# Joining the quarters of a Strassen-like MLP in PSUM, rectifying and squaring them on ScalarE, and spreading the modulation chunks anew

## What is computed

```python
def squared_relu_mlp(h, w_in, w_out):
    return jnp.square(jax.nn.relu(h @ w_in)) @ w_out
...
for i in range(DEPTH):
    ml = jnp.split((c_act @ w_mod[i] + b_mod[i])[:, None, :], 6, axis=-1)
    mc = jnp.split(cc_act @ w_mod[i] + b_mod[i], 6, axis=-1)
    ...
    xl = xl + ml[2] * yl
    xl = xl + ml[5] * squared_relu_mlp(modulate(xl, norm_mlp_g[i], ml[3], ml[4]), w_mlp_in[i], w_mlp_out[i])
    if not last:
        xc = xc + mc[5] * squared_relu_mlp(...)   # with the same weights
return rms_norm(xl, final_norm_g)
```

## Time and profile before

| | us |
|---|---|
| median of 3 runs | 1682.56 (1681.82 to 1687.36) |
| profiled execution | 1684.8 |
| its span | 1683.0 |
| PE busy | 1594.0 (95%) |
| DVE busy | 1084.3 (64%) |
| POOL busy | 741.1 (44%) |
| ACT busy | 568.6 (34%) |
| mean granted clock of PE | 0.979 |

### The profile page before, as it was taken

How to read it: one execution, slowest core, us unless ns; L and a number is a source line. 1 busy time by engine, 2 the same in 40 slices (tenths; PEclk the granted TensorE clock), 3 DMA queues, 4 the chain that set the end, 5 groups by cost and what they waited for, 6 DMA issues and landing times.

```text
span 1683.0 us, 23459 instructions
## 1 busy us (share of the span) xinstructions
PE 1594.0 (95%) x9272; PEld 1421.3 (84%) x9272; DVE 1084.3 (64%) x1390; ACT 568.6 (34%) x960; POOL 741.1 (44%) x451
## 2 busy tenths in 40 slices
PE   8999999994999898889979999999999999999998
PEld 5889888984989897889979888887888988888887
DVE  4697276269488888977885377707985653525264
ACT  4413365243122221213233241126883522222222
POOL 2421663243554545445474262434522644444442
PEclk9999999997999999999989999999999999999999
DMA  9482212221033342424322122211001232322221
GB/s 363 160 312 85 88 58 96 82 76 50 27 124 114 112 132 94 138 76 138 106 95 91 36 101 76 88 51 41 1 2 63 76 114 88 100 98 100 83 94 51
DMA packets 50344, 163.12 MB, mean 97 GB/s; under 512 B 6336, under 2 KB 8768, under 8 KB 46656
## 3 DMA queue, kind: packets, MB, share of 16 engines
q1 hardware_dynamic: 50240, 161.68, 28.4%
HBM read 158.78 MB, written 2.10 MB: 96 GB/s over the span
## 4 chain that ended last, share of the span: by engine, by line
PE 70%; DVE 20%; issue 6%; ACT 1%; DMA 1%; SPq 0%; POOL 0%; DVEq 0%; POOLq 0%; ACTq 0%
PE ps L2033 19%; PE ps L2034 19%; PE ps L2035 19%; DVE mod_acc L1405 7%; PE ps L2667 2%; PE ps L2629 2%; PE ps L2656 1%; DVE hidl L1654 1%; PE ps L2534 1%; PE ps L2522 1%; DVE mod_acc L1402 1%; PE ps L2562 1%; DVE xl L1626 1%; DVE hidl_f L1721 1%; PE ps L2346 1%
## 5 line engine op out<-in xcount | busy, mean ns | idle before, releaser
L725 POOL TENSOR_TENSOR w_lo<-raw,w_hi 128x1024 fp32r<-128x1024 f32 (+1 forms) x242 | 503.2, 2090 | 692.8 <-ACT w_hi L926 474.1
L2033 PE MATMUL ps<-h,w_hi 128*128 128x512 f32 (+2 forms) x1016 | 356.6, 351 | 3.6 <-DVE h L1654 1.7
L2034 PE MATMUL ps<-h,w_lo 128*128 128x512 f32 (+2 forms) x1016 | 354.2, 349 | 0.0
L2035 PE MATMUL ps<-h,w_hi 128*128 128x512 f32 (+2 forms) x1016 | 353.9, 348 | 0.0
L1626 DVE SCALAR_TENSOR_TENSOR xl<-ps,mods,xl 128x384 f32<-128x384 f32 (+2 forms) x144 | 73.1, 540 | 231.3 <-PE ps L2035 227.7
L2033 PEld LDWEIGHTS ps<-h,w_hi 128*128 128x128 f32 x1016 | 191.4, 188 | 28.1 <-issue 3.4
L2033 PE MATMUL ps<-hidl,w_hi 128*128 128x384 f32 (+2 forms) x448 | 159.3, 356 | 55.4 <-DVE hidl L1654 25.5
L2035 PEld LDWEIGHTS ps<-h,w_hi 128*128 128x128 f32 x1016 | 191.3, 188 | 17.0
L2034 PEld LDWEIGHTS ps<-h,w_lo 128*128 128x128 f32 x1016 | 191.4, 188 | 16.6
L926 ACT ACTIVATE w_hi<-raw 128x1024 fp32r<-128x1024 f32 x120 | 126.5, 1054 | 155.9 <-PE ps L2035 149.6
L1405 DVE SCALAR_TENSOR_TENSOR mod_acc<-mod_ring,cact,mod_acc 128x512 f32<-128x512 f32 x112 | 152.8, 1384 | 11.8 <-DVE mod_acc L1405 9.2
(11 more groups left out here) (300 smaller groups left out, 3231.5 us busy)
## 6 DMA issues: line engine op xcount, KB each, us to landing
raw<-units_dram SPq DMA_DIRECT2D x187, 512.0 KB, 3.4
mod_ring<-w_mod_dram SPq DMA_DIRECT2D x96, 256.0 KB, 2.8
mod_big<-w_mod_dram SPq DMA_DIRECT2D x16, 1024.0 KB, 10.3
mod_late<-w_mod_dram SPq DMA_DIRECT2D x8, 1024.0 KB, 8.5
xl<-x_dram SPq DMA_DIRECT2D x2, 2048.0 KB, 8.1
bias<-bias_dram SPq DMA_DIRECT2D x8, 384.0 KB, 3.8
xc<-ctx_dram SPq DMA_DIRECT2D x2, 1024.0 KB, 10.2
out_dram<-out_t SPq DMA_DIRECT2D x16, 128.0 KB, 1.9
```

What stands on the lines that cost most here:

```text
L725: ins = nc.gpsimd.tensor_tensor(w_lo[:, s, sl], src[:, sl], w_hi[:, s, sl].bitcast(F32), op=ALU.subtract)
L2033: mm(out, a[0], b[1], start=start, stop=False, skip_group_check=onto)
L2034: mm(out, a[1], b[0], start=False, stop=False, skip_group_check=onto)
L2035: return mm(out, a[0], b[0], start=False, stop=stop, skip_group_check=onto)
```

## The change

What it does:
- The chunks are made in the order 12 to 23. Blocks 1 to 4 make one each (all with vs 2), block 5 two, blocks 6 and 7 one each, the last units of the first MLP two (chunks 20 and 21), the first block of the second MLP two (22 and 23). In blocks 1 to 4, 4 steps stand ahead of `joined` for q0, step 4 and step 5 between the joins, and steps 6 and 7 with the split between tiles 0, 1 and 2.
- `joined` adds into PSUM (new `quarter_ps`), ACT rectifies and squares in place there and copies the high part out, and DVE subtracts from PSUM.
- In block 0, ACT rectifies three units before it copies, and DVE does more squares and lows ahead of the differences; the splits of the differences go between the tiles, and block 1 waits for each as it comes to it.
- `tail` has its extra product and extraction after the second half unit in place of the first.

```diff
-MOD_SEQ = [12, 16, 13, 17, 14, 18, 15, 19, 20, 21, 22, 23]
-MOD_OF = {b: [2 * b - 2, 2 * b - 1] for b in range(1, 6)} | {6: [10], 7: [11]}
+MOD_OF = {1: [0], 2: [1], 3: [2], 4: [3], 5: [4, 5], 6: [6], 7: [7]}
+MOD_LATE = {1: (10, (4, 5)), 2: (10, (6, 7)), 4: (11, (0, 1)), 5: (11, (2, 3)), 7: (11, (4, 5)), 8: (11, (6, 7))}
...
+        def quarter_ps(b, q):
+            bank = (4, 6, 2, 0)[q] if b < 7 else (0, 2, 6, 4)[q]
+            return ps[:, bank:bank + 2, 0:EVEN]
...  SP
-                if b < 6:
+                if b == 5:
                     load_mod(cs[1], (0, 1))
...
+                elif b < 5:
+                    for j in range(4, 8):
+                        load_unit(r + j)
+                load_mod(cs[-1] + 1, range(4))
+            for c in (8, 9):
+                for k in range(4 if c == 8 else 0, 8, 2):
+                    if c == 8 or k < 4:
+                        load_unit(M0 + LAST_R + 4 + (k - 4 if c == 8 else 4 + k) // 2)
+                    load_mod(c, (k, k + 1))
...
+            sp.wait_ge(unit_done, FIRST["out1"] + 1)
+            load_mod(10, range(4))
+            for i in range(16):
+                load_unit(raw_of(FIRST["mlp1"] + i) + SLOTS)
+                if i in MOD_LATE:
+                    load_mod(*MOD_LATE[i])
...  ACT, block 0
+                for i in range(3):
+                    first_relu(i)
+                for i in range(3):
+                    first_high(i)
+                first_relu(3)
+                first_high(3)
+                turn_high(0, h_hi[:, 0:4, H1], t1f[:])
...  ACT, blocks 1 to 7
                     def quarter_high(q):
+                        part = quarter_ps(b, q)
+                        if q < 3:
+                            act.wait_ge(s_added, 3 * (b - 1) + q + 1)
+                        else:
+                            act.wait_ge(unit_done, w + 7)
+                        nc.scalar.activation(part, part, ACT.Relu).then_inc(part_relu, 1)
+                        act.wait_ge(part_relu, n + q + 1)
+                        nc.scalar.activation(part, part, ACT.Square).then_inc(sq0_made, 1)
                         act.wait_ge(sq0_made, 4 * b + q + 1)
-                        nc.scalar.activation(quarter(b, q)[0], quarter(b, q)[2], ACT.Copy).then_inc(hq_hi, 1)
+                        nc.scalar.activation(quarter(b, q)[0], part, ACT.Copy).then_inc(hq_hi, 1)
...
                     for q in range(4):
-                        if q == 3:
-                            copy(0, 6, 3, ACT.Relu)
+                        quarter_high(q)
                         if b == 6 and q in (1, 2):
                             high_sum(7, q)
                         elif b != 6 or q == 0:
                             high_u(w + 7 + q)
-                        quarter_high(q)
...  DVE, block 0
                 first_square(0)
+                first_square(1)
+                first_square(2)
+                first_low(0)
                 dve.wait_ge(tf_made, 1)
                 difference(t3f[:], t4f[:], 1, H1, 0, H1)
-                first_low(0)
+                first_low(1)
+                first_low(2)
+                first_square(3)
                 less(t2f[:], t1f[:], 1, 1, H1)
+                first_low(3)
                 less(t4f[:], t2f[:], 3, 1, H0)
...  DVE, blocks 1 to 7 (joined)
-                        src = quarter(b, q)[2]
-                        tt(src, part_ps(b, side), src, op=ALU.add).then_inc(s_added, 1)
-                        dve.wait_ge(s_added, 3 * (b - 1) + q + 1)
-                        square(q, 4 * b + q, src)
+                        tt(quarter_ps(b, q), part_ps(b, side), quarter(b, q)[2], op=ALU.add).then_inc(s_added, 1)
...
-                    steps(c, range(6))
+                    early = 4 if b < 5 else 6
+                    steps(c, range(early))
                     joined(1, 3, 0)
-                    steps(c, range(6, 7))
+                    steps(c, range(early, early + 1))
                     low(0)
                     joined(0, 4, 1)
-                    steps(c, range(7, 8))
+                    steps(c, range(early + 1, early + 2))
                     low(1)
...
                     joined(1, 5, 2)
                     low(2)
-                    dve.wait_ge(s_copied, 4 * b)
-                    square(3, 4 * b + 3, quarter(b, 3)[2])
                     low(3)
-                    if b < 6:
+                    if b < 5:
+                        for m in range(8):
+                            add_tile(b, m)
+                            if m < 2:
+                                steps(c, range(6 + m, 7 + m))
+                            if m == 4:
+                                extract_late(c, 0)
...  DVE, last units of the first MLP
                     if m == 0:
-                        extract_late(11, 4)
+                        extract_late(7, 4)
+                        steps(8, range(4))
+                    elif m == 1:
+                        steps(8, range(4, 8))
+                    elif m == 2:
+                        extract_late(8, 4)
+                        steps(9, range(6))
...
+                steps(9, range(6, 8))
...  DVE, second MLP, first block
+                            if i == 5:
+                                extract_late(10, 6)
+                            elif i == 10:
+                                extract_late(11, 6)
+                            for k in (range(2 * i, 2 * i + 2) if i < 4 else {6: (0, 1, 2), 7: (3, 4, 5), 8: (6, 7)}.get(i, ())):
+                                mod_step(10 if i < 4 else 11, k)
...  PE
-                        if tile == 2 and b:
+                        if tile == 5 and 0 < b < 5:
                             mod_mm(MOD_OF[b][0], 0)
...
-                    if i == 0:
-                        mod_mm(MOD_OF[7][0], 4)
-                tail(2, u0 + 4, *hid_parts)
+                    if i in (0, 2):
+                        mod_mm(7 + i // 2, 4)
+                tail(2, u0 + 4, *hid_parts, lambda: mod_mm(9, 4))
...
+                        if first and i in (5, 10):
+                            mod_mm(10 if i == 5 else 11, 6)
```

More of the change, by code:

```diff
@@ L121, in loop @@
     @contextmanager
-    def loop(self, count, per):
-        base = self.n
-        with self.eng.Fori(0, count) as i:
+    def loop(self, first, end, per):
+        base = self.n - first * per
+        with self.eng.Fori(first, end) as i:
             self.n = base + i * per
             yield i
-        self.n = base + count * per
+        self.n = base + end * per
 def build(nc, t):
@@ L446, in mod_vs @@
         def mod_vs(c):
-            return 2 if MOD_SEQ[c] < 16 else 1
+            return 2 if c < 4 else 1
         HEAD_ORDER = [0, 2, 1, 3]
@@ L1643, in first_mlp @@
             def first_mlp():
-                def square(q, n, src):
-                    if n % 4 == 3 or n < 4:
-                        ins = tt(src, src, src, op=ALU.mult)
-                    else:
-                        ins = V.scalar_tensor_tensor(out=src, in0=src, scalar=0.0, in1=src, op0=ALU.max, op1=ALU.mult)
-                    ins.then_inc(sq0_made, 1)
-                def quarter_low(n, hi, lo, src):
-                    dve.wait_ge(hq_hi, n + 1)
-                    tt(lo, src, hi.bitcast(F32), op=ALU.subtract).then_inc(hq_made, 1)
                 def turn_low(j, lo, src, hi):
@@ L1675, in first_square @@
                     dve.wait_ge(relu0_made, i + 1)
-                    square(i, i, hidl_f[:, i])
+                    tt(hidl_f[:, i], hidl_f[:, i], hidl_f[:, i], op=ALU.mult).then_inc(sq0_made, 1)
                 def first_low(i):
-                    quarter_low(i, hidh[:, i], hidl[:, i], hidl_f[:, i])
+                    dve.wait_ge(hq_hi, i + 1)
+                    tt(hidl[:, i], hidl_f[:, i], hidh[:, i].bitcast(F32), op=ALU.subtract).then_inc(hq_made, 1)
                 dve.wait_ge(h_made, step(1, 1, KT - 1) + 1)
@@ L1710, in steps @@
                         mod_step(c, k)
-                for m in range(8):
+                add_tile(0, 0)
+                turn_low(0, h_lo[:, 0:4, H1], t1f[:], h_hi[:, 0:4, H1])
+                turn_low(1, t2l[:], t2f[:], t2h[:])
+                add_tile(0, 1)
+                add_tile(0, 2)
+                turn_low(2, t3l[:], t3f[:], t3h[:])
+                add_tile(0, 3)
+                add_tile(0, 4)
+                turn_low(3, t4l[:], t4f[:], t4h[:])
+                for m in range(5, 8):
                     add_tile(0, m)
@@ L1767, in blk @@
                         else:
+                            if first and i in (8, 12):
+                                dve.wait_ge(mod_done, PE_MODS + i // 4 + 9)
                             add_x(1, u + 16 * b + 1, u % 2, i - 8, 5, xa(1, b, i - 8))
@@ L1770, in blk @@
                                 sum_squares(4, i - 9)
-                with st.loop(HID_BLOCKS - 1, 8) as b:
-                    blk(b, False)
-                blk(HID_BLOCKS - 1, True)
+                        if first:
```

(23 more changed lines are left out.)

84 lines of the change are left out of this document (39 added, 45 removed).

## The result

The changed kernel took 1656.76 us (median of 4 runs, 1655.6 to 1657.48); the kernel before, run beside it, 1682.19. The ratio of the two is 0.9842, with a 95% interval of 0.9821 to 0.9862: faster by 1.6%. The prediction was 1653 with a range of 1626 to 1676. The profiled execution took 1657.24, its span 1655.5, 27.5 us less than before.

A forecast was written before the change was run, and what follows sets the result against it. PE bounds it, busy 1594.0 of 1683.0 us, so some 90 us of idle and half-clock losses can return. Terms sum to -29.3 on the profiled 1684.8: 1655.5, and 1653 after the 2.2 over the median; range 1626 to 1676.

The forecast's parts named there:

- Rival A: The sum of all terms: POOL's burst costs one tile wait a block, second MLP pays 13; 1653, chance 0.50.
- Blocks 1 to 4: First MLP: waits for `hidl` go, a tile wait of 5.1 comes; 70.0 a block, -22 in all, bounds -8 and -44.
- ACT in PSUM: Blocks 1 to 4: ACT instructions of 768 columns with input and output in PSUM take 0.82, bounds 0.8 to 1.0.
- The blocking of four lows, which now read PSUM: Blocks 1 to 4: lows reading PSUM are no longer blocked by POOL and take 0.95.
- rival E: Squares and lows in PSUM are not freed from POOL, DVE gains the squares alone; about 1671, chance 0.02.
- Block 0: Second products: the new order brings the last low 9.7 earlier; -9.5, bounds -6 and -14.
- Block 5: Keeps its modulation; its `hidl` wait of 2.6, with the dip 4.1, goes: -4.1 (-2 to -5).
- Block 6, the first last unit, chunks 20 and 21: Earlier split, block 6: -6.8; wait for q2 and q3 mostly goes, unit: -1.9; steps may hold chunk 21's product: +1.5.
- The second MLP: Chunks 22 and 23 land where DVE has nothing to spare; wait of 10.2 at chunk 22's product; +13.5, bounds +8 and +20.
- SP's queue doesn't enter: Load queue: where SP waits for a step it has units four ahead, so no time was booked for it.
- Rival B: Most blocking vanishes: step 7 ahead of POOL, block 65.5 (-18), second MLP +8 (-5.5); 1630, chance 0.28.
- rival D: Slower: POOL's burst already meets step 6 in blocks 1 to 4; 78.7 a block, 1688, chance 0.04.

The follow-up runs named there:

- joins-alone kernel: Kernel before with only the joins, squares and lows in PSUM, old block 0 order and old plan of chunks: 1672.0 us, ratio 0.9916.
- (a): Changed kernel with blocks 1 to 4's step 6 behind the third sum, step 7 behind the third low, split behind tile 0: 1632.33 us.
- (b): Changed kernel with blocks 1 to 4's step 6 behind the third sum, step 7 behind tile 0, split behind tile 1: 1628.97 us.

## Why the prediction was right, and where not

It said 1653, and 1656.8 came: on the profiled executions 1655.5 against 1657.24. The other 2 us are the 2.2 that it took off for the profiled execution of the kernel before; the one of the changed kernel is only 0.5 over its median. Rival A, the sum, is what happened. That the sum came out within 1.8 us of the measured change is in part luck, as block 0 was 1.8 better than forecast while block 5 and the second MLP were 1.4 and 2.2 worse. The terms, one by one.

- **Blocks 1 to 4.** Right in mechanism and size: -22 predicted, -22.0 measured, each between 69.5 and 70.8 us. `w_sum` was to start some 40 us into the block and did at 39.8; step 7 was to miss it by under 1 us and did by 0.4; the tile wait was to be 5.1 and was 4.6; the clock took 1.6 to 1.7 us in the two blocks that ran 3.41 us at 0.50, as forecast, and 2.7 to 2.9 in the two that ran 6.83 (PE busy 64.9 to 65.0 and 66.0 to 66.2, for 63.3 free). What the prediction didn't say is how the parts share it: the PSUM part alone brings 3.2 of the 22.0.
- **ACT in PSUM.** 0.82 was taken, with bounds of 0.8 and 1.0; it is 0.80. The join into PSUM was taken at 0.95 and is 0.96.
- **"The blocking of four lows, which now read PSUM".** The size (0.95) is right, the reason was not needed. With both operands from SBUF the time is the same, as all but one low of 24 now fall where POOL is idle. So the part of rival E that speaks of the lows would have cost next to nothing in this order.
- **Block 0.** -9.5 was undersized; it is -11.3 in the changed kernel and -10.6 by itself. PE began its last needed chunk at 407.80 (418.18 before), 10.4 earlier for 9.7, and 10.65 counted from the start of the stage; the rest is less time at the half clock (17.07 us of it for 27.31, PE busy 0.8 less). The order is what the prediction walked through: the first low at 393.5, the difference to 400.8 for 401.1, the last low at 407.7 for 408.5.
- **Block 5** was oversized: -4.1 predicted, -2.7 measured. The wait for `hidl` (2.57) and its dip did go. But PE then came earlier to tiles whose additions stand behind the second chunk's steps, and waits there of 0.81, 0.51 and 1.32 us became 0.88, 1.07, 1.21 and 1.44. The cover of one wait by another is the missed term, some 2 us (4.60 for 2.64). The joins-alone kernel shows the same 69.0.
- **Block 6, the first last unit, chunks 20 and 21**: -6.5, -2.0 and +1.0, for -6.8, -1.9 and +1.5. The split's wait fell from 10.74 to 4.55.
- **The second MLP** was undersized: +13.5 predicted, +15.7 measured. A single wait of 10.2 at the chunk's product was forecast, and waits of 2.62, 7.63 and 1.08 came, together 11.3, with 10.24 us at the half clock, of which PE was busy for 6.1, so that some 3 are lost, and the products. That the two chunks cost it is shown by the kernel that takes them away; that DVE has nothing to spare there is read from its timeline.
- **"SP's queue doesn't enter"** was wrong as a statement of fact. In the second MLP a unit's load stood behind loads that wait for a step, and ACT stood 9.87 us for it. It cost nothing that shows: with the order changed, the same time is lost at the chunk.
- **Rival B** (1630) needed step 7 ahead of the burst and a cheaper second MLP. The burst came 0.4 us too early for the first. Versions (a) and (b) took 1632 and 1629, near its time by another way: they leave the second MLP as it is, and in the four blocks they win 24 and 27 us for the 18 of that rival, as they move step 6 and the split too. The dips of the clock go with the waits. (The chances have a slip: rival D alone, at 1688, has 0.04, and slower has 0.03.)

The parts, from the spans of the runs: block 0's order 10.2 and the PSUM joins 15.7, together 25.9 of the 27.5. So the new plan of chunks as a whole is worth some 2 us: 18.8 in blocks 1 to 4, less 1.0 and 15.7 behind them.

## What to carry to other kernels

When work is moved from a crowded stage, price the stage that it lands in from its own idle time: here 18.8 us won were paid back with 16.7, while DVE stood idle for 55 us on end in an earlier stage of the same layer, where the same two chunks cost 0.8. Where two engines block each other, it isn't the count of instructions that decides but on which side of the other's burst they stand: four blocks' waits of 4.6 us went when the same instructions were queued a few places earlier. An order that holds by 0.4 us doesn't hold in every execution: in one run the burst came ahead of the whole step, and that wait was 6.62. A wait that goes exposes the next one behind it; list the small ones in the same stage before you book the whole of it.

## What the runs showed of the hardware

- ACT with input and output in the same PSUM tile, 128x768, takes 0.80 us; from PSUM into SBUF it takes 0.81, and from SBUF into SBUF 0.85. The place of its input and output costs at most 0.05 us here.
- DVE reading one operand from PSUM and one from SBUF takes as long as with both in SBUF: a low of 128x768 0.957 and 0.958 us.
- DVE's and POOL's instructions lengthen each other where they take turns: the cast 0.68 us free and 2.67 blocked, POOL's addition 2.40 free and up to 3.16 in the burst.
- With an order of work that leaves PE no gap, its granted clock stayed at 1.00, 2.4 GHz, over all 253.44 us of four blocks; with each wait of 4.6 us in the changed kernel came 3.41 or 6.83 us at 0.50, 1.2 GHz, from 0.4 to 1.7 us before the wait's end on. At 0.50 the matmuls of 384 columns started 0.32 us apart, at the full clock 0.17. The waits of 0.55 us in (a) had no such stretch behind them, and of the four of 2.06 to 2.58 us with step 7 behind tile 4 two had one and two had none, the longest among these.
